# A 576-token projection on one Trainium2 core: high and low parts of 256 tokens as one product of 512 columns in 79 tiles

## The reference, cut to what matters

```
h = RMSNorm(x)
[q_a|k_a|v_a|q_r|k_r|v_r|g_r|gate_a|gate_r] = h @ w_in        # 2048 -> 68 tiles of 128 features
br_a = attention(...) @ w_br_a ;  br_r = retention(...) @ w_br_r
x = x + (sigmoid(gate_a)*br_a + sigmoid(gate_r)*br_r) @ w_o   # 16 tiles
x = x + PEER(RMSNorm(x))       # query 16 tiles, scores of 16384 experts (128 tiles), values
x = x + sigmoid(RMSNorm(x) @ w_ple_gate) * (p @ w_ple_proj)   # 16 tiles each
```

## Time and profile before

| | |
|---|---|
| median of 3 runs | 4578.69 us (4576.86 to 4579.11) |
| span of the profiled execution | 4598.6 us (no other time of this execution is given) |
| PE busy | 4519.9 us, 98% of the span, 31465 matmuls |
| PE's share of the chain that ended last | 87% |
| DVE, ACT, POOL busy | 66%, 32%, 33% |
| granted TensorE clock, mean over the span | 0.991 of full |

### The profile page before, as it was taken

One profiled execution on the slowest core, in us unless ns is written; L12 is line 12 of the kernel. 1 busy time (PEld: TensorE's weight loads), 2 busy tenths in 40 slices (PEclk: granted clock), 3 DMA queues, 4 the chain that ended last, 5 costly groups with the idle time before them and its releaser, 6 DMA issues.

```text
span 4598.6 us, 79681 instructions
## 1 busy us (share of the span) xinstructions
PE 4519.9 (98%) x31465; PEld 4370.9 (95%) x31465; DVE 3019.9 (66%) x4190; ACT 1472.9 (32%) x2413; POOL 1495.7 (33%) x1076
## 2 busy tenths in 40 slices
PE   8999999999999999999999999999999999999998
PEld 8999999989999999988889999999999999999997
DVE  6643443334434779978883777664669989889843
ACT  4113332123323122267771121222233333332432
POOL 1000000010000004444443446243268777666311
PEclk9999999999999999999999999999999999999999
DMA  6555455455665545467777777776779899999522
GB/s 211 165 168 155 145 154 174 149 158 185 213 207 176 173 144 170 151 217 253 254 247 258 252 258 266 270 273 207 276 281 342 331 359 393 368 369 352 189 82 91
DMA packets 590447, 1044.65 MB, mean 227 GB/s; under 512 B 57633, under 2 KB 437809, under 8 KB 555441
## 3 DMA queue, kind: packets, MB, share of 16 engines
q1 hardware_dynamic: 230192, 510.99, 33.3%
q0 software_dynamic: 81808, 386.99, 22.5%
q10 hardware_dynamic: 278256, 144.08, 11.0%
HBM read 994.67 MB, written 274.86 MB: 276 GB/s over the span
## 4 chain that ended last, share of the span: by engine, by line
PE 87%; DVE 4%; DMA 3%; issue 2%; POOL 1%; ACT 1%; ACTq 0%; DVEq 0%; POOLq 0%; SPq 0%
PE PS L2326 55%; PE PS L2847 18%; PE PS L2350 10%; PE PS L2782 1%; DMA v_raw<-in_w 1%; DMA rows_y<-u_rows,sub_k 1%; DMA w_raw<-in_w 1%; DVE PS L2104 0%; POOL a_y L780 0%; DVE w_lo L1367 0%; PE PS L2726 0%; POOL a_el L830 0%; DMA rows_y<-v_rows,row_iy 0%; PE PS L2442 0%; ACT w_hi L896 0%
## 5 line engine op out<-in xcount | busy, mean ns | idle before, releaser
L2326 PE MATMUL PS<-h_hi,w_hi 128*128 128x288 f32 x6528 | 1955.3, 300 | 40.2 <-DVE w_lo L1367 25.0
L2326 PE MATMUL PS<-h_hi,w_lo 128*128 128x288 f32 x6528 | 1933.9, 296 | 0.0
L2326 PE MATMUL PS<-h_lo,w_hi 128*128 128x288 f32 x6528 | 1933.1, 296 | 0.0
L2326 PEld LDWEIGHTS PS<-h_hi,w_hi 128*128 128x128 f32 x6528 | 1235.1, 189 | 71.9 <-issue 36.1
L2326 PEld LDWEIGHTS PS<-h_lo,w_hi 128*128 128x128 f32 x6528 | 1235.8, 189 | 0.7
L2326 PEld LDWEIGHTS PS<-h_hi,w_lo 128*128 128x128 f32 x6528 | 1235.0, 189 | 0.0
L896 ACT ACTIVATE w_hi<-w_raw 128x1024 fp32r<-128x1024 f32 x444 | 470.6, 1060 | 1988.1 <-PE PS L2326 1904.8
L1367 DVE TENSOR_TENSOR w_lo<-w_raw,w_hi 128x1024 fp32r<-128x1024 f32 x404 | 499.0, 1235 | 722.9 <-ACT w_hi L896 718.8
L830 POOL DMA_INDIRECT a_el<-act_scr,act_i x192 | 336.4, 1752 | 59.1 <-issue 58.2
L2160 DVE SCALAR_TENSOR_TENSOR acc<-rows,a_sel,acc 128x2048 f32<-128x2048 f32 x128 | 301.3, 2354 | 7.4 <-DMA rows<-v_rows,row_i 4.6
L843 POOL DMA_INDIRECT rows<-v_rows,row_i x148 | 242.7, 1640 | 175.1 <-DVE acc L2160 101.1
(11 more groups left out here) (400 smaller groups left out, 7320.2 us busy)
## 6 DMA issues: line engine op xcount, KB each, us to landing
w_raw<-in_w SPq DMA_DIRECT2D x612, 512.0 KB, 4.7
v_rows<-in_w ACTq DMA_DIRECT2D x512, 256.0 KB, 3.9
v_raw<-in_w SPq DMA_DIRECT2D x128, 512.0 KB, 7.8
u_rows<-u_t SPq DMA_DIRECT2D x320, 128.0 KB, 3.6
act_scr<-gsp POOLq DMA_DIRECT2D x128, 288.0 KB, 4.2
gate_scr<-g_st POOLq DMA_DIRECT2D x12, 2048.0 KB, 8.4
k_raw<-in_w SPq DMA_DIRECT2D x40, 512.0 KB, 4.7
gates<-gate_scr SPq DMA_DIRECT2D x17, 768.0 KB, 7.3
```

The costliest lines, as they stand in the source:

```text
L2326: ins = mm(dst[:, a], w[:, m, at + n], xx[:, k, a * TH:(a + 1) * TH], start=first and n == 0 and r == 0, stop=last and n == len(ks) - 1 an ...
```

## The change

Every tile of 576 tokens is now cut into 256 + 320 tokens in place of 288 + 288. `across(b0)` gives the 576 columns as one run that begins in the middle of bank `b0` and ends at column 320 of the next. The arrays `h_lo` and `h_hi` become two planes of one array `h_two`, so that one access pattern can read both.

In 79 tiles (`apart=True`: feature tiles 5 to 27, the 40 spill tiles and the 16 output tiles), a k-step's first 256 tokens take two matmuls in place of three. One of 512 columns streams lo and then hi past `w_hi`, and its two results lie side by side in bank `b0`; one of 256 columns adds `w_lo @ h_hi` to the second. The other 320 tokens keep three matmuls. The two results must then be added by whoever empties the tile: DVE by a `tensor_reduce` over pairs (feature and spill tiles), or by a second addition into `x` (output tiles). All other tiles keep six matmuls in a k-step, now three of 256 and three of 320 columns.

```diff
-        def ring_a(t):
-            return PS[:, 2 * (t % 2):2 * (t % 2) + 2, 0:TH]
+        def across(b0):
+            return PS[:].rearrange("p b c -> p (b c)")[:, 512 * (b0 + 1) - TM:512 * (b0 + 1) - TM + T]
...
-                for a in range(2):
+                for c in (slice(0, TM), slice(TM, T)):
                     for n, k in enumerate(ks):
-                        for r, (w, xx) in enumerate(((wh, xh), (wh, xl), (wl, xh))):
-                            ins = mm(dst[:, a], w[:, m, at + n], xx[:, k, a * TH:(a + 1) * TH],
-                                     start=first and n == 0 and r == 0,
-                                     stop=last and n == len(ks) - 1 and r == 2)
+                        both, xh, xl = parts(k)
+                        opens, ends = first and n == 0, last and n == len(ks) - 1
+                        if c.start or not apart:
+                            mm(dst[:, c], wh[:, m, at + n], xh[:, c], start=opens, stop=False)
+                            mm(dst[:, c], wh[:, m, at + n], xl[:, c], start=False, stop=False)
+                        else:
+                            mm(PS[:, b0].rearrange("p (r t) -> p r t", r=2), wh[:, m, at + n], both[:, :, c],
+                               start=opens, stop=False)
+                        ins = mm(dst[:, c], wl[:, m, at + n], xh[:, c], start=False, stop=ends)
...
 # ACT, spilled(t)
-                nc.scalar.activation(halves(spill[:, t % 2]), ring_b(t), ACT.Copy).then_inc(s_free_b, 1)
+                act.wait_ge(S["lows"], t + 1)
+                nc.scalar.activation(spill[:, t % 2, TM:T], ring_b(t)[:, TM:T], ACT.Copy).then_inc(s_free_b, 1)
...
 # DVE, feature tiles 5 to 27
-                    v.tensor_copy(halves(dst), ring_f(f)).then_inc(s_free_a, 1)
+                    ch.did(v.tensor_reduce(dst[:, 0:TM], low_and_high(bank_f(f)), AX.X, ALU.add))
+                    v.tensor_copy(dst[:, TM:T], ring_f(f)[:, TM:T]).then_inc(s_free_a, 1)
+                    ch.wait()
...
+            def spilled_low(t):
+                dve.wait_ge(s_used, 2 * (N_FEAT + t) + 2)
+                if t >= 2:
+                    dve.wait_ge(S[f"spill{t % 2}"], 16 * (t // 2))
+                v.tensor_reduce(spill[:, t % 2, 0:TM], low_and_high(bank_b(t)), AX.X, ALU.add).then_inc(S["lows"], 1)
...
                 if s:
                     split(2 * N_FEAT + s + 1)
+                if s and s % 2 == 0:
+                    spilled_low(s // 2 - 1)
...
             split(B_BR + 1)
+            spilled_low(N_SPILL - 1)
...
 # DVE, add_output(j)
-                v.tensor_tensor(xt, xt, ring_a(j), ALU.add).then_inc(s_free_a, 1)
+                ch.did(v.tensor_tensor(xt, xt, ring_a(j), ALU.add))
+                ch.wait()
+                v.tensor_tensor(xt[:, 0:TM], xt[:, 0:TM], PS[:, bank_a(j), 0:TM], ALU.add).then_inc(s_free_a, 1)
```

More of the change, by code:

```diff
@@ L32 @@
 TH = T // 2
+TM = 256
 TT = 5
@@ L317, in build @@
         gn_var, gn_root = rms_m, rstd
-        (oa_hi, or_hi), e = run(rT, ("oa_hi", [P, 8, T], F32R), ("or_hi", [P, 8, T], F32R))
-        assert e <= rA + 34 * TB
-        oa_lo = at("oa_lo", [P, 8, T], F32R, rA)
-        or_lo = at("or_lo", [P, 8, T], F32R, rA + 10 * TB)
+        br_in = at("br_in", [P, 34, T], F32R, rA)
+        oa_lo, or_lo, oa_hi, or_hi = (br_in[:, n:n + 8] for n in (0, 10, N_KEEP, N_KEEP + 8))
         g_ab = at("g_ab", [P, 2, 2, T], F32, rA + 34 * TB)
@@ L2314, in _, with of_h, of_a, of_r @@
             mm = nc.tensor.matmul
-            def tile(dst, w, slot_k, xh, xl, ks, first, last, at=0):
+            def of_h(k):
+                return h_two[:, :, k], h_hi[:, k], h_lo[:, k]
+            def of_a(k):
+                return br_in[:, k:k + N_KEEP + 1:N_KEEP], oa_hi[:, k], oa_lo[:, k]
+            def of_r(k):
+                return br_in[:, 10 + k:N_KEEP + 9 + k:N_KEEP - 2], or_hi[:, k], or_lo[:, k]
+            def of_p(k):
+                return None, p_hi[:, k], p_lo[:, k]
+            def tile(b0, slot_k, parts, ks, first, last, at=0, apart=True):
+                dst = across(b0)
                 slot, m, kt = slot_k
@@ L2357, in counted_tile @@
                     for k in range(8):
-                        ins = tile(dst, None, ((b + s) % 2, 0, 8), h_hi, h_lo, [8 * s + k], s + k == 0, s * k == 7, at=k)
+                        ins = tile(b0, ((b + s) % 2, 0, 8), of_h, [8 * s + k], s + k == 0, s * k == 7, at=k,
+                                   apart=apart)
                         ins.then_inc(s_used if k == 7 else S["hk"], 1)
@@ L2412, in _ @@
                         pe.wait_ge(S["h_done"], KD + k + 1)
-                        ins = tile(ring_a(t), None, (0, 0, 8), h_hi, h_lo, [k], k == 0, False, at=k)
+                        ins = tile(bank_a(t), (0, 0, 8), of_h, [k], k == 0, False, at=k)
                     ins.then_inc(s_used, 1)
                 else:
-                    tile(ring_a(t), None, (0, 0, 8), h_hi, h_lo, range(8), True, False).then_inc(s_used, 1)
+                    tile(bank_a(t), (0, 0, 8), of_h, range(8), True, False).then_inc(s_used, 1)
                 if KR <= t - 2 < VR:
@@ L2424, in _ @@
                         pe.wait_ge(S["h_done"], KD + k + 1)
-                        ins = tile(ring_a(t), None, (1, 0, 8), h_hi, h_lo, [k], False, k == KD - 1, at=k - 8)
+                        ins = tile(bank_a(t), (1, 0, 8), of_h, [k], False, k == KD - 1, at=k - 8)
                     ins.then_inc(s_used, 1)
                 else:
-                    tile(ring_a(t), None, (1, 0, 8), h_hi, h_lo, range(8, KD), False, True).then_inc(s_used, 1)
+                    tile(bank_a(t), (1, 0, 8), of_h, range(8, KD), False, True).then_inc(s_used, 1)
             def a_scores(n):
@@ L2641, in _ @@
                 pe.wait_ge(s_lo, b + 1)
-                tile(ring_b(t), None, (s % 2, 0, 8), h_hi, h_lo, range(8 * (s % 2), 8 * (s % 2) + 4), s % 2 == 0, False)
+                tile(bank_b(t), (s % 2, 0, 8), of_h, range(8 * (s % 2), 8 * (s % 2) + 4), s % 2 == 0, False)
                 if s == 0:
@@ L2659, in _ @@
                     variances(h - 1)
-                tile(ring_b(t), None, (s % 2, 0, 8), h_hi, h_lo, range(8 * (s % 2) + 4, 8 * (s % 2) + 8), False,
+                tile(bank_b(t), (s % 2, 0, 8), of_h, range(8 * (s % 2) + 4, 8 * (s % 2) + 8), False,
                      s % 2 == 1, at=4).then_inc(s_used, 1)
@@ L2709, in query @@
                             pe.wait_ge(S["h_done"], 2 * KD + 8 * s + k + 1)
-                            ins = tile(ring_a(0), None, (s, 0, 8), h_hi, h_lo, [8 * s + k], s + k == 0, s * k == 7,
-                                       at=k)
+                            ins = tile(bank_a(0), (s, 0, 8), of_h, [8 * s + k], s + k == 0, s * k == 7,
+                                       at=k, apart=False)
                         ins.then_inc(s_used, 1)
@@ L2715, in query @@
                 elif t == KD - 1:
-                    counted_tile(ring_a(t), B_Q + 2 * t)
+                    counted_tile(bank_a(t), B_Q + 2 * t, apart=False)
                 else:
-                    full_tile(ring_a(t), B_Q + 2 * t, h_hi, h_lo, [(r, 4) for r in loops])
+                    full_tile(bank_a(t), B_Q + 2 * t, [(r, 4) for r in loops], apart=False)
             def scores(t, loops=(), bank=6):
@@ L2741, in plain @@
                 pe.wait_ge(s_free_b, at_step(N_SPILL + t - 1, [(r, 2) for r in loops]))
-                full_tile(ring_b(t), B_U + 2 * t, h_hi, h_lo, [(r, 4) for r in loops], None if t or loops else 3 * KD)
+                full_tile(bank_b(t), B_U + 2 * t, [(r, 4) for r in loops], None if t or loops else 3 * KD,
+                          apart=False)
             plain(0)
@@ L2892, in _ @@
                         pe.wait_ge(S["gx"], 2 * NQ + 11)
-                    tile(ring_a(m), None, (q % 2, m, 2), p_hi, p_lo, range(2), True, True
+                    tile(bank_a(m), (q % 2, m, 2), of_p, range(2), True, True, apart=False
                          ).then_inc(S["vt"] if m < 3 else s_used, 1)
-            full_tile(ring_b(0), B_PG + 4, h_hi, h_lo, h0=4 * KD)
+            full_tile(bank_b(0), B_PG + 4, h0=4 * KD, apart=False)
             pe.wait_ge(s_free_a, A_PG + KD // 2)
@@ L2899, in _ @@
             summed(ss[:])
-            full_tile(ring_b(1), B_PG + 6, h_hi, h_lo)
+            full_tile(bank_b(1), B_PG + 6, apart=False)
             with pe.Fori(1, KD // 2) as i:
```

87 lines of the change are left out of this document (49 added, 38 removed).

## The result

The changed kernel takes 4593.64 us against 4581.39 us of the kernel before (medians of 20 runs each). The ratio is 1.0025, 95% interval [1.0016, 1.0034]. By this ratio the changed kernel is 11.5 us slower (7.3 to 15.6); the medians themselves lie 12.25 us apart. The forecast was 4.2 us faster, with a range of 4560 to 4589 us.

The account below looks back on a forecast made before the run. TensorE, busy 4519.9 of 4598.6 us, was taken as the bound. The terms -11.6 + 4.8 + 0.4 + 1.8 + 0.4 = -4.2 us gave 4574.5 us from 4578.7, range 4560 to 4589.

Parts of the forecast that it names:

- five matmuls for six: In the 79 tiles, 1264 k-steps: each goes from 795.0 to 785.8 ns, -11.6 us (-13.5 to -10.4).
- mixing lengths costs: Rival, 79 tiles: 512 columns behind 256 take longer, +5.3 ns a k-step, 6.7 us; 4581.2 or 4589.3 us; chance 0.15.
- The new cut: In the other tiles, 2288 k-steps: each goes from 795.0 to 797.1 ns, +4.8 us (-5.5 to +11.7).
- VectorE's sums: Behind the last tiles: +0.4 us feature, +1.8 us spill, +0.4 us output; all other sums hidden.
- the new cut costs nothing: Rival, all 576-token tiles: long rows of 256 columns run at 117.5 ns, sum -16.4 us, 4562.3 us; chance 0.30.
- the fixed part isn't saved: Rival, all k-steps: equal columns give equal time, only DVE's 2.6 us is left, 4581.3 us; chance 0.05.
- DVE late in every spill slot: Rival, 40 spill tiles: each sum's 0.65 us is paid, 26 us slower, 4600 us; chance 0.03.
- The Trainium skill's 2.5 ns: Fixed cost of each matmul beyond its columns by that page: first term 3.2 us saved, second term nothing.

Follow-up runs that it names:

- The series with idle engines: Changed kernel with series of 48 matmuls added at its end, results unused: 256 columns 120.0 ns each, 512 in turn with 256 352.9 ns a pair.
- the one with groups and the early sum: 79 tiles with 512-column matmuls grouped first, others cut at 288, last spill sum ahead of DVE's split; against the kernel before: 4579.31 us, ratio 0.9986.

## Why the prediction was wrong

**The step that failed** first is *five matmuls for six*: "A k-step becomes 226.7 + 119 + 3 x 146.7 = 785.8 ns". The 226.7 was taken from 512 columns behind 512, but in the 79 tiles each of them stands behind 256. The pair takes 352.5 ns, the k-step 792.5, and the term is 1264 x -2.5 = -3.2 us instead of -11.6. That alone is 8.4 of the 15.7 us between forecast and result.

The prediction had this as its rival *mixing lengths costs*, from five periods of 232 ns in the earlier trace rows, and set it aside because VectorE was reading the banks there. The series with idle engines shows that this reason was wrong. The rival's size was nearly right, with some luck: +5.3 ns a k-step against 352.5 - 346.7 = 5.8 measured, though of the five periods that gave it only the first stands behind 256 columns and four stand behind 512. With 256 columns at 120 ns it gave +10.6 us, against 11.5 measured.

**The new cut** was right in sign and mis-sized: 119 ns for 256 columns is 120.0. A k-step of the other tiles costs 800, not 797.1, and the term is 2288 x 5.0 = +11.4 us by the periods instead of +4.8. The prediction had the right value as its upper end; one nanosecond decided it, as it had worked out. The burst of four in the earlier trace rows held the value: this row of the kernel before is its last two matmuls, up to the 512 columns at 1981.25.

```profile
1981.01 0.40 PE L2782 MATMUL PS<-oh_i,oh_j 128*128 128x256 f32 x2
```

They take 120 ns each; the mean of the four is lower because the first two, behind longer ones, take 0.23 us together. The new cut is now the largest term, and the kernel without it (288 elsewhere) shows no loss.

**VectorE's sums** were mis-sized too. As foretold came `br_t` with +1.9 us (+1.8), `stg` with +0.4 (+0.4), and the 40 spill sums hidden. The clock behind the wait for `br_t` is missing from the sum, 1.7 us in this profile. The feature tiles were to cost nothing but the last; PE already waited for `w_lo` in some of them, and these waits grew by 0.9 us. Behind the last output tile the prediction read a wait of 1.6 us for `h_lo`; that one lies at the start of the kernel. The wait there is for `ss`, and it grew by 0.7 us (0.4 foretold). Together that is 5.6 us in place of 2.6.

**The new sum** is -3.2 + 11.4 + 5.6 = +13.8 us by these rows, against 11.5 (7.3 to 15.6). The interval is too wide to tell it from the 10.8 that the 2.6 foretold would give, so the runs don't check the terms one by one.

The other rivals fell: *the new cut costs nothing* (120.0 ns in long rows), *the fixed part isn't saved* (with equal columns a k-step takes 792.5 ns with the joint product and 800 with six matmuls), *DVE late in every spill slot* (no such wait).

The Trainium skill's 2.5 ns ("TensorE: Matmul & The Clock Gate", section "Wait — 56ns, not 53.3ns?") is not borne out by the new series either: no series of one length came under 10 ns beyond its columns at the higher level. The 3 ns between 264 and 256 columns show that it isn't one constant either. That the first term came out at the 3.2 us which the prediction had estimated from this figure is chance: a joint product saves 13.3 ns a k-step, and the order takes back 5.8 and the dearer cut 5.0.

**What stays open.** By itself the new cut cost 9 us, twice measured, where the periods give 17.8. Here is part of it, in the rows of the later `plain` tiles (68 tiles, 1088 k-steps, 5.4 us by the periods). The kernel before:

```profile
2463.80:3364.20 900.40, 885.06 (x6626) 883.85 (x6625) 571.72 (x498) 189.18 (x216) 352.25 (x313) 0.99 0.74 251
```

The kernel with the new cut alone:

```profile
2468.00:3368.40 900.40, 886.83 (x6627) 885.95 (x6626) 572.67 (x498) 189.16 (x216) 351.47 (x313) 0.99 0.73 251
```

Equal to the tenth, with PE busier by 1.8 us and idle for that much less: its waits for `w_lo` in this stretch went from 15.3 to 13.6 us, which looks as if longer tiles filled waits that existed already. But one pair of profiles can't show that. Another kernel that keeps 288 here, the one with groups and the early sum, takes 4 us less:

```profile
2452.80:3349.20 896.40, 881.05 (x6626) 880.08 (x6625) 571.20 (x498) 189.16 (x216) 353.42 (x313) 0.99 0.74 252
```

Over all profiles the stretch takes 896.4, 898.9 and 900.4 us with 288 columns and 900.4 to 903.3 in seven with the new cut, 3.2 us more on average. By these ten profiles more than half of the 5.4 us arrives. Part of the rest is the clock. These are 10 us of the stretch, in the kernel before and with the new cut alone:

```profile
2774.00:2784.00 10.00, 9.05 (x56) 9.05 (x57) 8.65 (x11) 1.08 (x2) 8.17 (x7) 0.83 0.31 106
...
2778.00:2788.00 10.00, 9.40 (x73) 9.40 (x74) 9.85 (x13) 1.68 (x3) 8.17 (x7) 1.00 0.34 116
```

A granted clock of 0.83 costs 1.7 us there. The runs point the same way: their granted clock averages 0.9921 (35 runs) and 0.9923 (23) in the kernel before on the two chips, 0.9926 (11) and 0.9930 (12) with the new cut alone. That difference is worth 2 to 3 us of 4590, an estimate. The rest of the missing 9 us was not found. By the experiment, the step from 288 to the new cut in 2288 k-steps is 1.0025 - 0.9995 = 0.0030 or 13.8 us, with some 6 us of uncertainty. That is more a k-step than the 9 us on 3552 of them; the two readings are at the edge of what their intervals allow together.

## What to carry to other kernels

The price of a matmul is its period *in the order in which it will stand*: measure the pattern, not each length by itself, and not from the mean of a burst of four. Before products are joined, look at the cut: here a cut at 272 + 304 with all six matmuls beat 512 + 256 + 3 x 320 with five, without any sums. Where a change gains on the bound engine, look for the places where it must wait for another, and at the granted clock behind them: 7 of 18 us were given back at one wait of 5.4 us, and a wait that grew by 1.9 us cost 3.6 in five profiles of six. One profile of one execution can be off by more than the effect: compare several before a small difference is explained.
